# An attention loop whose blocks begin with the scores of the next but one, and a first tile set up in another order

## The chip, the cores and the metric

The kernel runs on one core of a Trainium2 chip. The metric is the device time of one launch in microseconds (us). The core's engines each work through their own instruction stream in order and wait for one another on semaphores: TensorE (PE, with its weight loads as PEld), VectorE (DVE), ScalarE (ACT), GpSimd (POOL) and the DMA queue of SyncE (SP).

## What is computed

Two encoder layers over 512 tokens and 16 learned meta tokens of width 1024. Each layer is wrapped in two gated feed-forward parts; layer 0 mixes by a short convolution and a state-space model, layer 1 by windowed attention with 16 heads, 4 key heads and a head width of 64. Cut to what matters here:

```
def swiglu(x, w_gate, w_up, w_down):
    return (jax.nn.silu(x @ w_gate) * (x @ w_up)) @ w_down

h = h + 0.5 * swiglu(rmsnorm(h, norm_ff1[layer]), ff1_w_gate[layer], ff1_w_up[layer], ff1_w_down[layer])
...
s_band = jnp.einsum('bnqhgd,bnshd->bhgnqs', qr, kb) - slopes * dist
s_meta = jnp.einsum('bnqhgd,bmhd->bhgnqm', qr, km)
probs = softmax_with_sink(jnp.concatenate([s_meta, s_band], axis=-1), sink)
o_real = (jnp.einsum('bhgnqm,bmhd->bnqhgd', probs[..., :N_META], vm)
          + jnp.einsum('bhgnqs,bnshd->bnqhgd', probs[..., N_META:], vb))
out = o_real.reshape(bsz, n_real, N_HEADS * HEAD_DIM)
return out.astype(hn.dtype) @ w_o
```

## The kernel before

Every dense product is made of three matmuls on split operands: a weight `w` becomes `wh` (rounded) and `wl = w - wh`, an input `x` becomes `xh` and `xl`, and PE sums `wh*xh + wh*xl + wl*xh`. A weight unit is 128x2048 values (16 blocks of 128x128). SP loads it into one of two `raw` slots, ACT makes `wh` (`split_high`, L1184), DVE makes `wl` (`split_low`, L1463), and the slot is loaded again when `wl` is done. Everything is written out by hand: the order of the calls in the source is the order in each engine's stream, and nothing overtakes within an engine.

**Start.** PE transposes the input tokens, DVE copies them into `h`. ACT sums the squares of the meta tokens and of the four token tiles (L1264, L1267), makes `wh` of the first tile's gate half (L1270), takes the roots of the sums (L1272), and makes the eight input slices `xh` (L1196), with `wh` of the up half (L1278) after the fifth. DVE makes `wl` of the gate half (L1569), the reciprocals and the eight `xl` (L1484). PE's `first_job` (L762) is the gate tile: 8 steps of k, 3 products each, as two matmuls of 264 columns; it waits for `xl(k)` before any product of step k. Then `first_scale` (L839) spreads the token norms, then the up tile. DVE copies the norms into `r` (L1583) and scales the gate tile into `t_a` (L1516), which frees the gate tile's banks for PE's third tile.

**Attention.** 16 blocks n = 0 to 15, four (j) for each key head (g). In block n before the change:

- PE: `probs_t(n)` transposes the normalised probabilities (L1097, L1098); `scores(n+2)` (L1086, L1087); then dense work, which is a quarter of the query projection of group g+2 (12 matmuls, L1045) while g+2 < 4, and from block 8 on the pieces of the output projection that `fill` names (`out_part(d, k0, k1)`, 3 matmuls of 512 columns for each k, L1141); then `values(n)` (L1108, L1110).
- DVE: `probs_meta(n)` copies the last transpose (L1866), `normed(n+1)` (L1854 to L1861), `softmax(n+2)` (scores and bias L1844, maximum L1848), `out_low(n)` (L1872). In blocks with j = 2 and g+2 <= 4 a whole `split_low` follows.
- ACT: `probs(n)` copies the four transposes (L1415), `exps(n+2)` (four exponentials, L1410), `out_high(n)` (L1420). In blocks 0, 4 and 8 a whole `split_high` follows.

What waits for what: `probs_t(n)` for `normed(n)`; `scores(n)` for the four L1844 of `softmax(n-1)`; `values(n)` for `probs(n)` and `probs_meta(n)`; `normed(n)` for `exps(n)`; `exps(n)` for `softmax(n)`; `out_high(n)` for `values(n)`; `out_low(n)` for `out_high(n)`. `scores(12)` also waits for a query norm that POOL makes from sums in block 8.

The second weight unit of the output projection (WO[0] + 1) is the one whose split falls in blocks 8 and 10; `out_part(2, ...)` in block 14 is the first to read it.

## Time and profile before

| | |
|---|---|
| median of 3 runs | 1949.73 us (1948.42 to 1950.04) |
| the profiled execution's own time | 1950.2 us |
| its span | 1948.1 us |
| PE busy | 1928.7 us, 99% of the span |
| DVE, ACT, POOL busy | 961.0, 604.7, 315.4 us |
| attention blocks 8 to 15 | 1493.33 to 1540.25 us of the span |

The span runs from the first to the last instruction of the profile; what is 2.1 us more in the time lies around it. A busy PE is not a PE at its peak, since a matmul's record lasts as long at half the clock as it needs there; the granted clock (PEclk, 1.00 is full speed) is a column of its own.

### The profile page before, as it was taken

What the parts mean: (1) busy time and instruction counts of PE and PEld (TensorE: products, weight loads), DVE (VectorE), ACT (ScalarE), POOL (GpSimd) and SP (SyncE); (2) the same over time, 40 slices, a digit from 0 to 9 for tenths busy, and PEclk for the clock granted to TensorE, in tenths of its full rate; (3) what the DMA queues carried; (4) which work ended last, traced back from release to release, by engine and by line L of the source; (5) the groups of instructions that cost most, each with busy time, mean ns of one, the idle gap of its engine ahead of it and who ended that gap; (6) DMA issues with size and microseconds to landing.
All of it is one profiled execution on the core that took longest, in us unless ns stands there. A gap on an engine that the chain in (4) does not pass through costs nothing.

```text
span 1948.1 us, 33853 instructions
## 1 busy us (share of the span) xinstructions
PE 1928.7 (99%) x13943; PEld 1813.2 (93%) x13943; DVE 961.0 (49%) x1059; ACT 604.7 (31%) x710; POOL 315.4 (16%) x568
## 2 busy tenths in 40 slices
PE   7999999999999999999999999999999999999999
PEld 7999999999999999999999999999877778888887
DVE  5444367566765443344554433445556554433443
ACT  5222222332243222222342222223455433222222
POOL 2888888001230000000000000000012000000000
PEclk9999999999999999999999999999999899999999
DMA  6322544455333322432243334322311133233323
GB/s 177 87 81 81 152 137 139 129 133 130 96 88 87 86 81 82 118 87 70 79 111 86 82 86 113 87 70 81 108 44 44 44 108 87 78 95 108 101 70 89
DMA packets 329026, 185.61 MB, mean 95 GB/s; under 512 B 7288, under 2 KB 322968, under 8 KB 328952
## 3 DMA queue, kind: packets, MB, share of 16 engines
q1 hardware_dynamic: 323280, 166.81, 30.8%
q0 software_dynamic: 5344, 17.69, 3.2%
q8 instruction: 53, 0.87, 0.2%
q14 instruction: 21, 0.17, 0.0%
q10 hardware_dynamic: 328, 0.07, 0.0%
HBM read 173.56 MB, written 9.80 MB: 94 GB/s over the span
## 4 chain that ended last, share of the span: by engine, by line
PE 96%; DVE 2%; ACT 1%; issue 0%; ACTq 0%
PE ps L729 78%; PE ps L948 5%; PE ps L990 2%; PE ps L1045 2%; PE ps L1009 1%; PE ps L1173 1%; PE ps L1141 1%; ACT arena L1410 1%; DVE wl L1463 0%; PE ps L770 0%; DVE arena L1844 0%; PE ps L1110 0%; PE ps L1108 0%; PE ps L1086 0%; PE ps L883 0%; PE ps L909 0%
## 5 line engine op out<-in xcount | busy, mean ns | idle before, releaser
L729 PE MATMUL ps<-xl,wh 128*128 128x264 f32 (+1 forms) x2448 | 567.1, 301 | 0.0
L729 PE MATMUL ps<-xh,wh 128*128 128x264 f32 (+1 forms) x2448 | 565.9, 301 | 0.1
L729 PE MATMUL ps<-xh,wl 128*128 128x264 f32 (+1 forms) x2448 | 565.7, 301 | 0.0
L1463 DVE TENSOR_TENSOR wl<-raw,wh 128x2048 fp32r<-128x2048 f32 x173 | 411.1, 2376 | 169.8 <-ACT wh L1184 169.6
L729 PEld LDWEIGHTS ps<-xh,wh 128*128 128x128 f32 x2448 | 392.3, 188 | 16.9 <-issue 0.7
L1184 ACT ACTIVATE wh<-raw 128x2048 fp32r<-128x2048 f32 x173 | 329.6, 1905 | 246.7 <-PE ps L729 211.3
L729 PEld LDWEIGHTS ps<-xl,wh 128*128 128x128 f32 x2448 | 391.3, 188 | 15.7 <-issue 0.2
L729 PEld LDWEIGHTS ps<-xh,wl 128*128 128x128 f32 x2448 | 391.0, 188 | 14.9
L729 PE MATMUL ps<-act_l,wh 128*128 128x264 f32 (+1 forms) x1232 | 284.7, 301 | 0.0
L729 PE MATMUL ps<-act_h,wh 128*128 128x264 f32 (+1 forms) x1232 | 284.6, 301 | 0.0
L729 PE MATMUL ps<-act_h,wl 128*128 128x264 f32 (+1 forms) x1232 | 284.3, 301 | 0.0
L1519 DVE TENSOR_TENSOR t_c<-ps,r 128x528 f32<-128x528 f32 (+1 forms) x88 | 61.9, 703 | 371.7 <-PE ps L729 371.6
L729 PEld LDWEIGHTS ps<-act_h,wh 128*128 128x128 f32 x1232 | 197.4, 188 | 7.7
L729 PEld LDWEIGHTS ps<-act_l,wh 128*128 128x128 f32 x1232 | 196.8, 188 | 7.5
L729 PEld LDWEIGHTS ps<-act_h,wl 128*128 128x128 f32 x1232 | 196.6, 188 | 7.5
L1224 ACT ACTIVATE act_h<-t_c 128x528 f32 (+3 forms) x88 | 56.6, 643 | 461.9 <-DVE t_c L1522 461.9
L310 POOL TENSOR_TENSOR arena<-arena 128x32 f32<-128x32 f32 (+7 forms) x245 | 186.3, 760 | 24.8 <-DMA ssm_tables<-arena 5.8
L613 POOL TENSOR_SCALAR arena<-arena 128x16 f32<-128x16 f32 x4 | 1.0, 258 | 899.2 <-DVE arena L1832 863.6
L1499 DVE SCALAR_TENSOR_TENSOR h<-ps,h 128x528 f32 (+2 forms) x72 | 50.7, 704 | 192.6 <-PE ps L729 184.4
L1222 ACT ACTIVATE t_bs<-t_a 128x528 f32<-128x528 f32 (+1 forms) x88 | 56.5, 642 | 282.6 <-DVE t_a L1516 282.6
L1524 DVE TENSOR_TENSOR act_l<-t_c,act_h 128x528 f32 (+3 forms) x88 | 68.6, 779 | 78.9 <-ACT act_h L1224 78.9
L1522 DVE TENSOR_TENSOR t_c<-t_c,t_bs 128x528 f32<-128x528 f32 (+1 forms) x88 | 68.5, 778 | 9.0
(296 smaller groups left out, 1684.0 us busy)
## 6 DMA issues: line engine op xcount, KB each, us to landing
raw<-in_ff_w_gate SPq DMA_DIRECT2D x88, 512.0 KB, 4.0
raw<-in_ff_w_up SPq DMA_DIRECT2D x88, 512.0 KB, 5.2
raw<-in_ff_w_down SPq DMA_DIRECT2D x64, 384.0 KB, 4.0
raw<-in_ff_w_down SPq DMA_DIRECT2D x64, 320.0 KB, 3.7
raw<-in_even_w_in SPq DMA_DIRECT2D x16, 512.0 KB, 5.2
raw<-in_attn_w_qkv SPq DMA_DIRECT2D x12, 512.0 KB, 4.6
raw<-in_even_w_out SPq DMA_DIRECT2D x8, 512.0 KB, 4.6
raw<-in_attn_w_o SPq DMA_DIRECT2D x8, 512.0 KB, 4.7
```

The lines of the kernel that those rows point to most:

```text
L310: did(g.tensor_tensor(o, x, y, op))
L729: last = nc.tensor.matmul(ps[:, 2 * pair + hf, 0:nh], w[:, slot, b * P:(b + 1) * P], x[:, k0 + k, c0 + hf * nh:c0 + (hf + 1) * nh], start= ...
L948: last = nc.tensor.matmul(ps[:, 2 * (p % 2) + hf, 0:L // 2], w[:, slot, b * P:(b + 1) * P], x[:, k, hf * L // 2:(hf + 1) * L // 2], start= ...
L990: last = nc.tensor.matmul(ps[:, 2 * (d % 2) + hf, 0:L // 2], w[:, slot, b * P:(b + 1) * P], x[:, k, hf * L // 2:(hf + 1) * L // 2], start= ...
L1184: nc.scalar.activation(wh[:, c % 2, :], raw[:, c % 2, :], ACT.Copy).then_inc(wh_ready, 1)
L1222: nc.scalar.activation(t_b[:, cols], t_a[:, cols], ACT.Silu).then_inc(silu_done[n], 1)
L1224: nc.scalar.activation(act_h[:, s + 2 * i, cols], t_c[:, cols], ACT.Copy).then_inc(act_h_done[n], 1)
L1463: v.tensor_tensor(wl[:, c % 2, :], raw[:, c % 2, :], wh[:, c % 2, :].bitcast(F32), ALU.subtract).then_inc(wl_ready, 1)
L1499: v.scalar_tensor_tensor(hd, tile(pair, col), scale, hd, ALU.mult, ALU.add).then_inc(tile_evac, 1)
L1519: v.tensor_tensor(halves(t_c, col), tile(1, col), halves(r, col), ALU.mult).then_inc(tile_evac, 1)
L1522: v.tensor_tensor(t_c[:, cols], t_c[:, cols], t_b[:, cols], ALU.mult).then_inc(gated[n], 1)
L1524: v.tensor_tensor(act_l[:, s + 2 * i, cols], t_c[:, cols], act_h[:, s + 2 * i, cols].bitcast(F32), ALU.subtract).then_inc(act_ready[n], 1)
```

## The change

Three things, none of which adds or removes a matmul.

1. **Block order.** PE begins block n with `scores(n+2)`, then a first piece of dense work (`fill`, only in blocks 9 and 12 to 15), then `probs_t(n)`, then the query quarter or the second dense piece (`cover`), then `values(n)`. Blocks 8, 10 and 11 have only the second piece. DVE runs `softmax(n+2)` ahead of `normed(n+1)`; ACT runs `out_high(n)` ahead of `exps(n+2)`.
2. **Split of unit WO[0] + 1.** ACT makes it in two halves at the ends of blocks 8 and 9, DVE in four quarters at the ends of blocks 9 to 12.
3. **First tile.** The gate half is loaded with a semaphore of its own. ACT makes its `wh` before the last square, starts the `xh` slices at once, and takes the roots only after `wh` of the up half. DVE makes `wl` in pieces of 2 and 6 blocks around the first `xl`. PE starts step k on `xh(k)` alone and waits for `xl(k)` only ahead of the second product. `first_scale` moves into the middle of the up tile.

```diff
             def first_job(col):
...
-                pe.wait_ge(gate_split[1], 1)
+                pe.wait_ge(gate_split[0], 1)
                 for k in range(KD):
-                    pe.wait_ge(x_ready, k + 1)
+                    pe.wait_ge(xh_done, k + 1)
                     for q, (w, x) in enumerate(((wh, xh), (wh, xl), (wl, xh))):
+                        if q == 1:
+                            pe.wait_ge(x_ready, k + 1)
+                        if q == 2 and k in (0, EARLY):
+                            pe.wait_ge(gate_split[1], 1 if k == 0 else 2)
...
+            def second_job(col):
...
+                pe.wait_ge(wh_ready, 1)
+                for k in range(KD):
+                    if k == KD // 2:
+                        first_scale()
...
                                 first_job(col)
-                                first_scale()
-                                pe.wait_ge(wl_ready, 1)
+                                second_job(col)
+                                continue
...
-            fill = {8: [(0, 0, 2)], 9: [(0, 2, 4)], 10: [(1, 0, 1)], 11: [(1, 1, 2)], 12: [(1, 2, 4)], 13: [(0, 4, 6)], 14: [(2, 0, 4)], 15: [(1, 4, 6), (2, 4, 6)]}
+            fill = {9: [(0, 2, 3)], 12: [(1, 2, 3)], 13: [(0, 4, 5)], 14: [(2, 0, 2)], 15: [(1, 4, 6)]}
+            cover = {8: [(0, 0, 2)], 9: [(0, 3, 4)], 10: [(1, 0, 1)], 11: [(1, 1, 2)], 12: [(1, 3, 4)], 13: [(0, 5, 6)], 14: [(2, 2, 4)], 15: [(2, 4, 6)]}
             for n in range(NB):
                 g, j = divmod(n, NT)
-                probs_t(n)
                 if n + 2 < NB:
                     scores(n + 2)
+                for d, k0, k1 in fill.get(n, ()):
+                    out_part(d, k0, k1)
+                probs_t(n)
                 sums = g + 1 if j == 0 and g + 1 < NKV else None
                 if g + 2 < NKV:
                     query_part(g + 2, j // 2, j % 2, sums)
-                for d, k0, k1 in fill.get(n, ()):
+                for d, k0, k1 in cover.get(n, ()):
                     out_part(d, k0, k1, sums)
                 values(n)
...
+            def half_high(hf):
+
+                c, at = WO[0] + 1, slice(hf * UNITW // 2, (hf + 1) * UNITW // 2)
+                act.wait_ge(raw_landed[c % 2], 32 * (c // 2 + 1))
+                act.wait_ge(tile_full, j0 + 2 * NKV)
+                nc.scalar.activation(wh[:, c % 2, at], raw[:, c % 2, at], ACT.Copy).then_inc((half_split, wh_ready)[hf], 1)
...
+                out_high(n)
                 if n + 2 < NB:
                     exps(n + 2)
-                out_high(n)
-                if n % NT == 0 and g + 2 <= NKV:
+                if n % NT == 0 and g + 2 < NKV:
 
                     split_high(u0 + 4 + (g + 1) % 2, (g + 1) // 2, j0 + 2 * (g + 2))
+                if n in (NB // 2, NB // 2 + 1):
+                    half_high(n - NB // 2)
...
+                if n + 2 < NB:
+                    softmax(n + 2)
                 if n + 1 < NB:
                     normed(n + 1)
-                if n + 2 < NB:
-                    softmax(n + 2)
...
-                if j == 2 and g + 2 <= NKV:
+                if j == 2 and g + 2 < NKV:
                     split_low(u0 + 4 + (g + 1) % 2, (g + 1) // 2)
+                if NB // 2 < n <= NB // 2 + 4:
+                    quarter_low(n - NB // 2 - 1)
```

Where the streams differ, three places. The first is ACT's stream at the start of the program, from the square of the meta tokens to the norms' diagonals (`t_c`). Before:

```order
15 L1264 ACTIVATE act_l,tok<-arena 16x2x512
16 L1267 ACTIVATE act_l,tok<-arena 128x2x512 x4
17 L1270 ACTIVATE wh<-raw 128x1024
18 L1272 ACT_TABLE_LOAD
19 L1272 ACTIVATE tok<-tok 128x4
20 L1273 ACTIVATE tok<-tok 16x1
21 L1196 ACTIVATE xh<-h,vec 128x528 x5
22 L1278 ACTIVATE wh<-raw 128x1024
23 L1196 ACTIVATE xh<-h,vec 128x528 x3
24 L1281 ACTIVATE t_c<-ident,tok 128x128 x4
```

And in the changed kernel (L1226 is the `xh` slice, L1304 and L1311 the two halves of `wh`):

```order
16 L1299 ACTIVATE act_l,tok<-arena 128x2x512 x3
17 L1304 ACTIVATE wh<-raw 128x1024
18 L1226 ACTIVATE xh<-h,vec 128x528
19 L1299 ACTIVATE act_l,tok<-arena 128x2x512
20 L1226 ACTIVATE xh<-h,vec 128x528 x7
21 L1311 ACTIVATE wh<-raw 128x1024
22 L1313 ACT_TABLE_LOAD
23 L1313 ACTIVATE tok<-tok 128x4
24 L1314 ACTIVATE tok<-tok 16x1
25 L1317 ACTIVATE t_c<-ident,tok 128x128 x4
```

The fourth square, the table load and both roots went behind the input slices. The second place is ACT's stream in blocks 9 and 10 (`arena<-ps` is `probs`, `arena<-arena` the exponentials, `act_h<-ps` is `out_high`). Before, from `probs(9)` on:

```order
392 L1415 ACTIVATE arena<-ps 128x512
393 L1410 ACTIVATE arena<-arena 128x145 x4
394 L1420 ACTIVATE act_h<-ps 128x2x128
395 L1415 ACTIVATE arena<-ps 128x512
396 L1410 ACTIVATE arena<-arena 128x145 x4
397 L1420 ACTIVATE act_h<-ps 128x2x128
```

And in the changed kernel, from `probs(9)` to `probs(10)` and a little around them (L1451 is `probs`, L1456 `out_high`, L1446 the exponentials, L1464 half a split):

```order
390 L1456 ACTIVATE act_h<-ps 128x2x128
391 L1446 ACTIVATE arena<-arena 128x145 x4
392 L1464 ACTIVATE wh<-raw 128x1024
393 L1451 ACTIVATE arena<-ps 128x512
394 L1456 ACTIVATE act_h<-ps 128x2x128
395 L1446 ACTIVATE arena<-arena 128x145 x4
396 L1464 ACTIVATE wh<-raw 128x1024
397 L1451 ACTIVATE arena<-ps 128x512
```

`probs(n)`, for which `values(n)` waits, now stands behind four exponentials and, in blocks 9 and 10, behind half a split. The third place is DVE's stream in block 10 (`arena<-ps` 128x128 is `probs_meta`, `act_l<-ps` is `out_low`). Before:

```order
628 L1866 COPY arena<-ps 128x128
629 L1854 RECIPROCAL arena<-arena 128x4
630 L1860 TENSOR_TENSOR t_c<-arena 128x512
631 L1861 TENSOR_TENSOR arena<-arena 128x4x17
632 L1844 SCALAR_TENSOR_TENSOR arena<-ps,arena 128x145 x4
633 L1848 TENSOR_REDUCE arena<-arena 128x4
634 L1872 TENSOR_TENSOR act_l<-ps,act_h 128x2x128
635 L1463 TENSOR_TENSOR wl<-raw,wh 128x2048
636 L1866 COPY arena<-ps 128x128
```

And in the changed kernel:

```order
632 L1918 COPY arena<-ps 128x128
633 L1896 SCALAR_TENSOR_TENSOR arena<-ps,arena 128x145 x4
634 L1900 TENSOR_REDUCE arena<-arena 128x4
635 L1906 RECIPROCAL arena<-arena 128x4
636 L1912 TENSOR_TENSOR t_c<-arena 128x512
637 L1913 TENSOR_TENSOR arena<-arena 128x4x17
638 L1924 TENSOR_TENSOR act_l<-ps,act_h 128x2x128
639 L1934 TENSOR_TENSOR wl<-raw,wh 128x512
640 L1918 COPY arena<-ps 128x128
```

The softmax went ahead of the normalising, and what stands between `out_low(10)` and `probs_meta(11)` is a quarter of the split instead of the whole.

## Rows read from the trace of the kernel before

**Rows 1.** Chain that ended last: shares by engine; one piece (start, us, line, count).

```profile
PE 96%; DVE 2%; ACT 1%; issue 0%; ACTq 0%
...
1531.24 2.78 PE ps L1141 x12
```

**Rows 2.** PE's waits: line, releaser, us in total, times, longest.

```profile
PE ps L770 <- DVE xl L1484: 6.6, 1, 6.6
PE ps L1108 <- DVE arena L1866: 3.3, 1, 3.3
...
PE ps L1108 <- issue: 0.8, 1, 0.8
PE ps L1086 <- DVE arena L1844: 0.5, 1, 0.5
```

**Rows 3.** Blocks 8, 12, 15: busy us of PE, PEld, DVE, ACT, POOL; PEclk.

```profile
1493.33:1499.81 6.48, 6.48 (x58) 5.42 (x56) 4.24 (x12) 2.60 (x11) 0.00 (x0) 1.00 0.50 138
...
1518.28:1525.79 7.51, 7.51 (x41) 5.91 (x39) 3.48 (x11) 4.16 (x18) 0.00 (x0) 0.58 0.32 89
...
1535.40:1540.25 4.85, 4.85 (x31) 3.75 (x30) 0.62 (x2) 0.98 (x2) 0.00 (x0) 1.00 0.00 0
```

**Rows 4.** Timeline of PE, block 10: start, duration, line, operation.

```profile
1505.56 0.66 PE L1097 MATMUL ps<-ident,t_a 128*128 128x128 f32 x4
...
1506.26 0.50 PE L1086 MATMUL ps<-arena 64*128 64x128 f32 x4
...
1507.28 0.50 PE L1141 MATMUL ps<-act_h,wh 128*128 128x512 f32 x1
...
1508.09 0.38 PE L1108 MATMUL ps<-arena 128*128 128x128 f32 x2
...
1509.56 0.66 PE L1097 MATMUL ps<-ident,t_c 128*128 128x128 f32 x4
```

**Rows 5.** Timeline of DVE, blocks 10 and 11.

```profile
1507.54 0.28 DVE L1866 COPY arena<-ps 128x128 f32<-128x128 f32 x1
...
1508.68 1.19 DVE L1844 SCALAR_TENSOR_TENSOR arena<-ps,arena 128x145 f32<-128x145 f32 x4
1509.90 0.76 DVE L1848 TENSOR_REDUCE arena<-arena 128x4 f32<-128x580 f32 x1
...
1513.04 2.28 DVE L1463 TENSOR_TENSOR wl<-raw,wh 128x2048 fp32r<-128x2048 f32 x1
```

**Rows 6.** Timeline of ACT, block 10: first exponential, copy of block 11.

```profile
1510.69 0.42 ACT L1410 ACTIVATE arena<-arena 128x145 f32<-128x145 f32 x1 [3.05 <-DVE arena L1848]
...
1512.57 0.58 ACT L1415 ACTIVATE arena<-ps 128x512 f32<-128x512 f32 x1
```

**Rows 7.** Timeline of ACT and DVE at the start.

```profile
12.12 1.04 ACT L1267 ACTIVATE act_l<-arena 128x1024 fp32r<-128x1024 f32 x1
...
13.15 1.04 ACT L1270 ACTIVATE wh<-raw 128x1024 fp32r<-128x1024 f32 x1
...
15.71 3.23 ACT L1196 ACTIVATE xh<-h,vec 128x528 fp32r<-128x528 f32 x5
...
16.46 3.48 DVE L1484 SCALAR_TENSOR_TENSOR xl<-h,vec,xh 128x528 fp32r<-128x528 f32 x5 [0.41 <-ACT xh L1196]
...
21.66 1.26 ACT L1281 ACTIVATE t_c<-ident,tok 128x128 f32<-128x128 f32 x4
...
27.98 0.71 DVE L1516 TENSOR_TENSOR t_a<-ps,r 128x528 f32<-128x528 f32 x1
...
33.14 0.71 DVE L1519 TENSOR_TENSOR t_c<-ps,r 128x528 f32<-128x528 f32 x1 [4.45 <-PE ps L729]
```

**Rows 8.** Columns of rows 3: first tile; query projection; blocks 9 to 11.

```profile
17.30:22.50 5.20, 5.13 (x23) 5.16 (x24) 4.61 (x7) 5.20 (x10) 4.92 (x7) 0.50 0.88 151
...
1425.30:1428.70 3.40, 3.40 (x10) 2.67 (x11) 1.69 (x3) 2.49 (x3) 2.18 (x10) 0.54 0.00 0
...
1503.20:1512.20 9.00, 8.19 (x72) 6.07 (x72) 5.32 (x16) 4.67 (x19) 1.08 (x5) 1.00 0.00 0
```

More of the change, by code:

```diff
@@ L29 @@
 UNITW = BLK * P
+EARLY = 2
 def trunk_program(nc, a, out, stop=None):
@@ L764, in first_job @@
                 c0, nh, nb = col
-                pe.wait_ge(gate_split[1], 1)
+                pe.wait_ge(gate_split[0], 1)
                 for k in range(KD):
-                    pe.wait_ge(x_ready, k + 1)
+                    pe.wait_ge(xh_done, k + 1)
                     for q, (w, x) in enumerate(((wh, xh), (wh, xl), (wl, xh))):
+                        if q == 1:
+                            pe.wait_ge(x_ready, k + 1)
+                        if q == 2 and k in (0, EARLY):
+                            pe.wait_ge(gate_split[1], 1 if k == 0 else 2)
                         for hf in range(nb):
                             last = nc.tensor.matmul(ps[:, hf, 0:nh], w[:, 0, k * P:(k + 1) * P], x[:, k, c0 + hf * nh:c0 + (hf + 1) * nh],
+                                                    start=(k == 0 and q == 0), stop=(k == KD - 1 and q == 2))
+                last.then_inc(tile_full, 1)
+            def second_job(col):
+                c0, nh, nb = col
+                pe.wait_ge(wh_ready, 1)
+                for k in range(KD):
+                    if k == KD // 2:
+                        first_scale()
+                    for q, (w, x) in enumerate(((wh, xh), (wh, xl), (wl, xh))):
+                        if k == 0 and q == 2:
+                            pe.wait_ge(wl_ready, 1)
+                        for hf in range(nb):
+                            last = nc.tensor.matmul(ps[:, 2 + hf, 0:nh], w[:, 0, (KD + k) * P:(KD + k + 1) * P], x[:, k, c0 + hf * nh:c0 + (hf + 1) * nh],
                                                     start=(k == 0 and q == 0), stop=(k == KD - 1 and q == 2))
@@ L1273, in _ @@
             nc.scalar.activation(tok[0:META, 0, NT:NT + 1], tok[0:META, 0, NT:NT + 1], ACT.Sqrt).then_inc(sd_ready, 1)
-            act.wait_ge(init_evac, NT + 2)
-            for d in range(KD):
-                scaled_high(0, d, ALL)
-                if d == KD // 2:
-                    nc.scalar.activation(wh[:, 0, GW:2 * GW], raw[:, 0, GW:2 * GW], ACT.Copy).then_inc(wh_ready, 1)
             act.wait_ge(tok_r, 2)
@@ L1572, in _ @@
             v.reciprocal(tok[0:META, 1, NT:NT + 1], tok[0:META, 0, NT:NT + 1]).then_inc(tok_r, 1)
-            for d in range(KD):
-                scaled_low(0, d, ALL)
-            dve.wait_ge(wh_ready, 1)
-            v.tensor_tensor(wl[:, 0, GW:2 * GW], raw[:, 0, GW:2 * GW], wh[:, 0, GW:2 * GW].bitcast(F32), ALU.subtract).then_inc(wl_ready, 1)
             dve.wait_ge(init_evac, NT + 2)
@@ L1873, in out_low, with quarter_low @@
                                 cols(act_h).bitcast(F32), ALU.subtract).then_inc(ol_done, 1)
+            def quarter_low(q):
+                c, at = WO[0] + 1, slice(q * UNITW // 4, (q + 1) * UNITW // 4)
+                if q < 2:
+                    dve.wait_ge(half_split, 1)
+                else:
+                    dve.wait_ge(wh_ready, c + 1)
+                low = v.tensor_tensor(wl[:, c % 2, at], raw[:, c % 2, at], wh[:, c % 2, at].bitcast(F32), ALU.subtract)
+                if q == 3:
+                    low.then_inc(wl_ready, 1)
             dve.wait_ge(prep, count["att_consts"])
```

41 lines of the change are left out of this document (33 added, 8 removed).

## The prediction

> **What bounds the kernel now.** I read the chain of work that ended last first: 96% of it is PE [rows 1], so a change pays only where PE waits or runs at half its clock. The waits of PE are few [rows 2]: 6.6 us for the first `xl`, and in the attention loop 3.3 us in block 11 (`values(11)` for `probs_meta(11)`), 0.8 us in block 9, 0.5 us in block 0. The third view is the granted clock by stretches: 0.50 while the first tile runs [rows 8], and 0.58 in block 12 [rows 3]. Everything else on PE is dense and unchanged, since no matmul is added or removed. So the whole question is how much of these waits and slow stretches goes, and what new waits the new orders make.
>
> **Attention, what goes.** The 3.3 us: DVE starts a whole `split_low` at 1513.04, 2.28 us long, behind `out_low(10)`, and `probs_meta(11)` stands behind it [rows 5]. The quarters take about 0.65 us each (a quarter of 2.28 plus a fixed part), so the wait goes. It costs a second time: after it PE is at 1.2 GHz instead of 2.4. Block 12 takes 7.51 us [rows 3], and its parts at full clock are transposes 0.70, scores 1.02, three dense matmuls 0.81 (six: 0.81 + 3 x 0.23 = 1.50, with 2.78 / 12 = 0.23 for one [rows 1]), values 1.47 [rows 4], together 4.69; that is 2.8 us, and `values(11)` ahead of it, 2.7 us at half speed by the same ratio, lose 1.2. The 0.8 us of block 9 were ACT's whole `split_high` ahead of `probs(9)`; as two halves of 1.04 us (the same copy of 1024 columns [rows 7]) at the ends of blocks 8 and 9 it comes back below. What can go: 3.35 + 0.84 + 4.0 = 8.2 us.
>
> **Attention, what comes.** (a) Block 0. PE now begins with `scores(2)`, which need the four L1844 of `softmax(1)`. They were 0.5 us late when 0.7 us of transposes stood ahead [rows 2, 4]; now the transposes stand behind, and nothing covers: the wait is about 1.2 us, 0.75 more.
>
> (b) ACT. `values(n)` waits for `probs(n)`, and ahead of that ACT now has `out_high(n-1)` and four exponentials, both after `values(n-1)`. These take 1.88 us (1510.69 to 1512.57) and `probs` 0.58 [rows 6]. With 0.1 us until ACT sees `values(n-1)` and 0.05 back to PE, that is 2.6 us from the end of one `values` to the start of the next. PE has, in between, in blocks 10 and 11: scores 1.02, transposes 0.70, three matmuls 0.81 = 2.53, so 0.1 us is missing; in blocks 9, 12, 13 with the first dense piece 3.34, nothing missing; in blocks 1 to 7 a quarter query projection of 12 matmuls (0.81 + 9 x 0.23 = 2.9) makes 4.6, and even in blocks 1 and 5, where a whole `split_high` (about 1.9 us) comes too, ACT's 2.6 + 1.9 = 4.5 just fits. The half splits do not fit: 2.6 + 0.95 = 3.55 against 3.34 in block 9 (0.2 missing) and against 2.53 in block 10 (1.0 missing). Sum: 0.2 + 1.0 + 0.1 = 1.3 us, say 1.4.
>
> (c) DVE. Its block is `probs_meta` and `normed` 1.14 (1507.54 to 1508.68), `softmax` 1.2 + 0.7 [rows 5], `out_low` 0.35, a quarter 0.6: 4.0 us with nothing waited for, against PE's 4.0 us in blocks 10 and 11 (1505.56 to 1509.56) [rows 4]. After `probs_meta(n)` DVE needs 2.9 us until `normed(n+1)` is done; PE then has `values(n)` 1.47 and `scores` 1.02 ahead of the transposes that need it, plus what it waited for ACT (0.3 or more), so about even. I put nothing on it and keep 0.5 us for the range. In blocks 0 to 7 PE's 6.1 us cover it.
>
> (d) More, smaller groups. The first matmul of a dense group takes 0.12 us longer than the others (0.81 for three [rows 4] against 0.23 each [rows 1]). Five blocks (9, 12 to 15) have one group more: 0.5 us.
>
> (e) POOL: `scores(12)` come 0.7 us earlier in their block; the norm for them needs about 5 us from the end of block 8's dense work, and PE gets there 6.4 us later (values 1.5, block 9 4.9). Hidden. `wl` of the second unit is ready in block 12, read in block 14; its slot is loaded two blocks later and read at the end of the output projection. Hidden by some 25 us.
>
> Attention: 8.2 - 0.75 - 1.4 - 0.5 = **5.6 us**. If ACT's and DVE's gaps all close, 7; if they double, 3.7.
>
> **Start.** ACT: the third square ends and the gate copy starts at 12.12 instead of 13.15 [rows 7]; it ends at 13.15, the first `xh` (3.23 / 5 = 0.65 us) at 13.8, the fourth square at 14.8, seven more `xh` at 19.3, the up half of `wh` at 20.3. The table load and the roots take what lay between the gate copy and the first `xh` before, 15.71 - 14.19 = 1.5 us, and DVE's reciprocals 0.3 more, so `t_c` starts at about 22.1 instead of 21.66. The gate half must have landed by 12.1; in the trace its copy starts straight behind the squares, and it is the first load after the tokens, so I take it as landed. PE: `wh*xh(0)` at 13.8 instead of 17.37; `xl(0)` at 14.5; `xh(1)` at 15.4, `xl(1)` at 16.2; from there on ACT and DVE deliver a step each 0.7 us, and PE is the slower one while its clock is half: before, four steps took the 5.2 us of the slow stretch [rows 8], 1.3 us a step, and 0.73 at full clock (six matmuls of 0.23 x 264 / 512 = 0.12). So steps 0 and 1 are done at 17.1 at half clock, or 16.7 at full, against 20.0 before. Then it hangs on when the clock rises. Before, it rose 5.2 us after the matmuls began. In the query projection it was at half for 3.4 us of dense matmuls [rows 8] and then full. From the dense stream's start at 16.2 that gives 19.6 to 21.4; I take 19.5, because sparse work from 13.8 on lies ahead of it. Then 1.8 steps are done at half by 19.5, and 4.2 x 0.73 = 3.1 remain: the gate tile ends at 22.5 instead of 25.5, **3.0 us** earlier. At 22.7 it would be 24.0, 1.5 us; with no fall at all `xl(7)` (20.4) bounds it.
>
> The up tile follows without a wait (`wh` 20.3, `wl` 21.6) and holds the 1.4 us of `first_scale` that stood in front of it; `t_c` is complete at 23.7, needed at 25.4. The next bound is the third tile, which needs the gate tile scaled into `t_a`. Before, that came 6.3 us after the start of `t_c` (21.66 to 27.98), through ACT's and DVE's split of the next unit, and no PE wait lies in it. It will be at 28.4, done at 29.1. The third tile starts after the up tile at 22.5 + 5.85 + 1.4 = 29.8 instead of at about 32.9 (DVE is released at 33.14 [rows 7]). So 3.0 us is kept, and 3.8 is the most there can be. Behind it PE is dense for hundreds of us, so the gain stays.
>
> **A page that speaks against it.** Between dense pieces PE will have values, scores and transposes in one row, with short waits. Blocks 9 to 11 had just that with a wait of 0.84 us, and the granted clock stayed at 1.00 up to 1512.2 [rows 8]. The Trainium skill, "TensorE: Matmul & The Clock Gate", section "A second HAM failure mode: psum-queue depth-cycling", says that a PE which idles briefly but often between groups of matmuls lets its clock oscillate between half and full. By the page blocks 9 to 13 would be partly slow, and the sum would be worth 4 us less or worse; by the row it stands.
>
> **Sum.** 5.6 + 3.0 = 8.6 us from a time of 1950.2 us for the profiled execution (span 1948.1): 1941.6. The median is 0.5 below that execution, so **1941.1 us**, -0.44%. A measurement of this kernel can tell about 0.2% (3.9 us) from no change. The likeliest case alone runs from 1939.5 (start 3.6, attention 6.6) to 1944.1 (start 1.5, attention 4.1).
>
> **Rivals.**
> 1. *The clock falls once in the thinned stretch or behind block 0's 1.2 us wait.* For it: before the query projection PE waited for nothing and still ran at 0.54 behind transposes and two-column matmuls; block 0 now has 1.2 us of waiting and 1.7 of small matmuls in a row. Against: rows 8, blocks 9 to 11. Price: as in blocks 11 and 12, 4.0 us: 1945.1. Chance 0.14.
> 2. *The early start is lost.* The sparse products do not count, and the clock rises at 22.7 or later, as before. For it: the clock was at 0.50 when the first tile began. Attention is unchanged: 5.6 + 0.5 to 1.5, 1942.6 to 1943.6. Chance 0.11.
> 3. *The wait moves to `normed`.* DVE's softmax stands ahead of it, and each of blocks 9 to 13 makes the transposes wait. By (c) the loop of DVE is 4.0 us, as long as PE's; with 0.6 us of semaphores in each of five blocks that is 3 us: 1944. Against: the exponentials are done before DVE comes to them. Chance 0.06.
> 4. *Slower: the clock falls in block 9 and does not come back until block 13's end.* A slow block took 7.51 against 4.69, 1.6 times. Blocks 9 to 13 hold 4.8 + 4.0 + 4.0 + 4.8 + 4.8 = 22.4 us of PE work; 0.6 of that is 13.4, less the 1.4 of waits that disappear in it: 12 us lost, 8.6 gained, 1953. It decides from 14 us of PE work at half clock on. For it: only 0.8 to 1.6 us of each 4 to 5 is dense. Against: block 10 had as little and kept 1.00. This is what the page's rule would do here at its worst. Chance 0.04.
> The forecast itself has 0.65.
>
> **Range and chances.** 1938.5 to 1946 holds the forecast, rivals 2 and 3 and most of rival 1. Below 1945.8 lie the forecast, rivals 2 and 3 and some two thirds of rival 1, less what I may have overlooked: faster 0.85, within 0.2% 0.10, slower 0.05.
>
> **What would show it.** In the changed trace: L1135 in block 11 without a wait of more than 0.3 us and clock 1.00 in blocks 11 and 12; a wait of about 1 us ahead of `values(10)` with `probs` as its releaser, 0.2 in block 9; a wait of about 1.2 us for `scores(2)`; blocks 8 to 15 in 40.5 us instead of 46.9; the first product at 13.8; PE at full clock by 20; the up tile's release of DVE at about 30. Wrong if the gate half lands after 12.1, if blocks 1 and 5 wait for `probs` (0.1 us of margin), or if the clock falls where it did not.

## The result, and the profile after

On the same chip the changed kernel took **1937.97 us** (median of 6 runs, 1937.42 to 1941.06) and the kernel before 1949.93 us (6 runs, 1948.42 to 1951.09): ratio 0.9941, 95% interval 0.9928 to 0.9954. The forecast was 1941.1 us with a range of 1938.5 to 1946, so the median lies 0.5 us below the range. The direction and most parts were right; the gain was 12.0 us where 8.6 was summed. The profiled execution after took 1938.08 us, its span is 1936.3 (before 1950.2 and 1948.1).

The shares of the chain that ended last, and PE's waits (line, releaser, us in total, times, longest), which answer to [rows 1, 2]:

```profile
PE 98%; DVE 1%; ACT 0%; DMA 0%; issue 0%; SPq 0%
```

```profile
PE ps L782 <- ACT xh L1226: 2.2, 1, 2.2
PE ps L1135 <- issue: 1.7, 3, 1.1
...
PE ps L1113 <- DVE arena L1896: 1.1, 1, 1.1
```

The 3.3 us of block 11 are gone. `values` (L1135) waits three times, 0.4 us in block 9, 1.1 in block 10, 0.2 in block 11; the forecast had 0.2, 1.0 and 0.1. Block 0's wait is 1.1 us, where 1.2 was forecast. "issue" hides the releaser here, and the timeline of ACT, from `out_high(9)` to `probs(10)`, names it (start, duration; L1456 is `out_high`, L1464 half the split, L1451 `probs`); the last line is PE's `values(10)`:

```profile
1499.74 0.38 ACT L1456 ACTIVATE act_h<-ps 128x256 fp32r<-128x256 f32 x1 [1.76 <-PE ps L1137]
...
1501.62 1.05 ACT L1464 ACTIVATE wh<-raw 128x1024 fp32r<-128x1024 f32 x1
1502.57 0.58 ACT L1451 ACTIVATE arena<-ps 128x512 f32<-128x512 f32 x1
...
1503.24 0.46 PE L1135 MATMUL ps<-arena 128*128 128x128 f32 x2 [1.14 <-issue]
```

`probs` ends at 1503.15 and `values(10)` starts at 1503.24. In experiment 7, where no half split stands there, block 10 takes 4.22 us instead of 5.16.

Stretches of PE: first tile mostly at half clock, then the rest of the first two tiles, the query projection, the end of block 9 with most of block 10, and block 12 (columns as in rows 3):

```profile
14.40:18.30 3.90, 3.66 (x15) 3.17 (x16) 3.87 (x8) 3.90 (x7) 3.90 (x5) 0.56 0.85 150
18.30:29.70 11.40, 11.40 (x93) 11.21 (x93) 7.71 (x12) 8.59 (x15) 4.42 (x6) 1.00 0.78 170
1422.40:1428.05 5.65, 5.65 (x26) 4.33 (x26) 1.69 (x3) 2.37 (x3) 3.27 (x15) 1.00 0.00 0
...
1498.90:1504.90 6.00, 4.86 (x46) 3.51 (x45) 5.32 (x15) 3.40 (x11) 0.00 (x0) 1.00 0.00 0
...
1509.10:1513.90 4.80, 4.76 (x41) 3.52 (x41) 3.83 (x12) 2.58 (x10) 0.00 (x0) 1.00 0.00 0
```

Block 12 is at 1.00 and takes 4.8 us, where it took 7.51 at 0.58 [rows 3]. In the query projection the clock is 1.00, where it was 0.54 for 3.4 us [rows 8]; the change edits nothing in that stretch, and the forecast had counted on no difference.

PE's and ACT's timelines at the start:

```profile
14.40 0.48 PE L782 MATMUL ps<-xh,wh 128*128 128x264 f32 x2 [2.25 <-ACT xh L1226]
15.12 0.81 PE L782 MATMUL ps<-xl,wh 128*128 128x264 f32 x2 [0.24 <-DVE xl L1529]
...
22.43 0.41 PE L797 MATMUL ps<-xh,wh 128*128 128x264 f32 x2
...
25.35 1.05 PE L870 MATMUL ps<-t_c,ones 128*128 128x128 f32 x8
...
29.70 0.48 PE L737 MATMUL ps<-xh,wh 128*128 128x264 f32 x2
```

```profile
11.81 1.04 ACT L1304 ACTIVATE wh<-raw 128x1024 fp32r<-128x1024 f32 x1
13.52 0.73 ACT L1226 ACTIVATE xh<-h,vec 128x528 fp32r<-128x528 f32 x1 [0.67 <-DVE vec L1608]
...
19.59 1.05 ACT L1311 ACTIVATE wh<-raw 128x1024 fp32r<-128x1024 f32 x1
...
22.53 1.28 ACT L1317 ACTIVATE t_c<-ident,tok 128x128 f32<-128x128 f32 x4 [0.28 <-DVE tok L1628]
```

The first product comes at 14.40 (forecast 13.8), since ACT waits 0.67 us for DVE's copy of the vectors. The clock is full from 18.3 on (19.5), the gate tile ends at 22.43 (22.5), `t_c` starts at 22.53 (22.1), and the third tile starts at 29.70 (29.8). That the gate tile ends on time is two errors that cancel: the first product came 0.6 us later than forecast, and the full clock 1.2 us earlier.

**Where the 11.8 us of span went.** From the start times of PE's pieces in the two timelines (before, after):

| stretch | before | after | gained |
|---|---|---|---|
| start to the key transposes | 1422.23 | 1419.20 | 3.03 |
| key transposes to `scores(0)` | 10.32 | 8.78 | 1.54 |
| `scores(0)` to `scores(1)` | 4.02 | 4.01 | 0.01 |
| `scores(1)` to the end of block 0 | 12.39 | 12.89 | -0.50 |
| blocks 1 to 7 | 44.37 | 43.30 | 1.07 |
| blocks 8 to 15 | 46.85 | 40.28 | 6.57 |

A block ends here where the next piece of PE starts, so blocks 8 to 15 before are 46.85 us and not the 46.9 that runs to the end of `values(15)`. The sum is 11.72. Two lines were not in the forecast at all: 1.54 in the query projection and 1.07 in blocks 1 to 7.

### The profile page after: what moved, and what is told of

It is laid out like the page before. It is cut to its first block, busy times and chain, and to the rows that moved or that the text cites. A ratio compares the mean times of both kernels' runs of the same rounds, so it can differ in the third digit from the quotient of the medians.

```text
span 1936.3 us, 33860 instructions
## 1 busy us (share of the span) xinstructions
PE 1922.4 (99%) x13943; PEld 1808.8 (93%) x13943; DVE 959.7 (50%) x1063; ACT 605.2 (31%) x711; POOL 317.6 (16%) x568
## 4 chain that ended last, share of the span: by engine, by line
PE 98%; DVE 1%; ACT 0%; DMA 0%; issue 0%; SPq 0%
PE ps L737 78%; PE ps L975 5%; PE ps L1017 2%; PE ps L1072 2%; PE ps L1036 1%; PE ps L1168 1%; PE ps L1203 1%; PE ps L1135 1%; PE ps L1137 1%; PE ps L1113 1%; PE ps L1124 0%; PE ps L782 0%; PE ps L910 0%; PE ps L936 0%; PE ps L935 0%; PE ps L926 0%
## 5 line engine op out<-in xcount | busy, mean ns | idle before, releaser
L1220 ACT ACTIVATE t_bs<-h 128x528 f32 (+1 forms) x40 | 25.7, 644 | 147.8 <-DVE h L1544 129.4
```

## The experiments

Medians are of the runs beside the kernel before on the same chip; a gain read from a stretch is from the profiled execution.

**1. The kernel before, unchanged.** How far do executions differ?

> The kernel before, unchanged, to see the granted clock of several executions. Theory A (the fall of the clock behind the key transposes is a matter of chance and of when PE gets there): at least one of its executions shows it missing, its mean clock is then 0.996 instead of 0.995 and its time about 1.6 us lower. Theory B (the change itself took it away): every execution has it, and the 24 matmuls of the second query half take 7.3 us as in the first profile, never 5.7.

1949.94 us (10 runs, 1947.43 to 1950.40), ratio 0.9999 (0.9990 to 1.0009). The 27 runs of the kernel before on that chip reach from 1947.31 to 1951.27, with none between 1948.9 and 1949.4. So a single profiled execution can stand 2 us above or below another of the same kernel. In the profile the query projection's clock fell again. Three of the ten executions lie at 1947.4 to 1948.2 with a mean clock of 0.996, as theory A wants; but three at 1949.8 to 1950.3 have 0.996 too, so the times alone don't settle it. The profiles of 2, 3 and 4 do: they have no fall, and 3 and 4 keep the start of before.

**2. The start alone.** `first_job`, `second_job`, the loads and the streams of ACT and DVE at the start; the attention loop of before.

```
+            def second_job(col):
...
-                pe.wait_ge(gate_split[1], 1)
+                pe.wait_ge(gate_split[0], 1)
```

> The first tile's new order alone. My sum: 3.0 us faster than before (the trace of the changed kernel shows the third tile 3.15 us earlier); a rival that the early products bring no earlier clock gives 0.5 to 1.5 us. The attention loop keeps its waits of 3.3, 0.8 and 0.5 us and its half clock of 9 us. If the clock behind the key transposes depends on the moment at which PE arrives there, this run may have lost that fall too and be 4.6 us faster.

1946.82 us (1944.93 to 1948.59), 2.8 us below the median before. Stretches from the first product to full clock, and of blocks 11 and 12:

```profile
13.50:19.00 5.50, 4.86 (x22) 4.18 (x23) 5.47 (x10) 5.50 (x10) 5.50 (x6) 0.69 1.01 198
...
1511.70:1520.30 8.60, 8.59 (x40) 6.54 (x41) 6.13 (x18) 2.71 (x11) 0.00 (x0) 0.50 0.44 123
```

The start's gain stands by itself, and the 3.3 us wait with half the clock behind it stays in the attention loop. In the profile the key transposes start 2.3 us earlier than in the kernel before, not 3.0.

**3. The order of the blocks alone.** PE's, ACT's and DVE's order of the changed kernel, with the whole splits of before.

```
-                probs_t(n)
                 if n + 2 < NB:
                     scores(n + 2)
+                for d, k0, k1 in fill.get(n, ()):
+                    out_part(d, k0, k1)
+                probs_t(n)
```

> The block order of all three engines alone, with the unit's split still whole at the ends of blocks 8 (ACT) and 10 (DVE). By the streams: block 0 waits 1.1 us; blocks 1 to 7 gain 1.1 us, since a dense group behind transposes costs 0.2 us less than one behind the scores; the wait in block 9 is about 1.1 us, in block 11 about 0.9, and neither is long enough for the clock to fall: 6 us faster than before. A rival that the whole split alone makes the long wait (3.3 us) and the fall behind it gives at most 2 us.

1942.33 us (1941.39 to 1943.08), ratio 0.9965 (0.9952 to 0.9977). Blocks 8 to 15 take 41.1 us, and their clock is 1.00. The whole split costs `values` one wait of 1.2 us and one of 1.0, instead of 3.3 and a slow stretch. The medians give the order 7.3 us. The stretches give it 6.3: 5.8 in blocks 8 to 15 and 1.05 in blocks 1 to 7, less 0.5 in block 0, where 6 was expected.

**4. The splits alone.** Halves and quarters, orders and start of before.

```
+                if n in (NB // 2, NB // 2 + 1):
+                    half_high(n - NB // 2)
...
+                if NB // 2 < n <= NB // 2 + 4:
+                    quarter_low(n - NB // 2 - 1)
```

> The halves and quarters alone, all streams in the order of before. The loop through DVE and ACT then has a period of 5.5 us a block (the copies of the last transposes stood at 1496.5, 1502.0 and 1507.5), and PE has 4.0 us of work in blocks 10 and 11 and 4.7 in 12 and 13: waits of about 1 us each stay in blocks 11 to 13, but no long one, and the clock stays at 1.00: 4 us faster. A rival that the whole split is all that was wrong gives 7 us or more.

1948.53 us (1945.80 to 1949.53), ratio 0.9995 (0.9986 to 1.0005). A miss: it was expected some 4 us faster. PE's wait (L1109 is `values`, L1876 `probs_meta`), the stretch from `values(10)` to the end of block 11's scores, and ACT's first exponential of block 9:

```profile
PE ps L1109 <- DVE arena L1876: 4.5, 4, 1.7
```

```profile
1506.10:1516.70 10.60, 8.92 (x69) 6.24 (x69) 6.51 (x18) 4.37 (x20) 0.00 (x0) 0.84 0.01 2
```

```profile
1502.56 0.42 ACT L1411 ACTIVATE arena<-arena 128x145 f32<-128x145 f32 x1 [2.12 <-DVE arena L1858]
```

The 3.3 us wait did not go, it was dealt out: 4.5 us in four blocks. Nor did the clock stay at 1.00, as was expected: behind the longest of these waits, 1.7 us ahead of `values(11)`, it was 0.50 from 1512.2 to 1515.6. Blocks 8 to 15 take 45.5 us, 1.4 less than before. With the old order ACT's exponentials wait for a softmax that stands behind DVE's `normed`, and `out_high`, the half split and `probs` wait behind them. In the kernel before, the whole `split_low` was only what stood visibly in front of `probs_meta`.

**5. The changed kernel again**, as the base of 6 to 8, on another chip.

> The changed kernel once more. The kernel before falls into two groups of times, about 1947.9 and 1950.2 us, and the second is the one in which the clock falls behind the key transposes. If that fall is chance in any kernel, the changed kernel has the same two groups about 10 us lower, near 1937.9 and 1940.2. If the change takes the fall away, there is one group near 1937.9 alone.

1940.51 us (1939.55 to 1941.82), kernel before 1949.05, ratio 0.9954 (0.9938 to 0.9971). The waits are those of the first profile. But in the query projection the clock fell:

```profile
1422.60:1425.90 3.30, 3.30 (x10) 2.62 (x10) 1.69 (x3) 2.50 (x3) 2.07 (x10) 0.50 0.00 0
1425.90:1429.90 4.00, 4.00 (x19) 2.97 (x17) 0.00 (x0) 0.00 (x0) 1.23 (x6) 0.99 0.00 0
```

From the sums to `scores(0)` it took 9.09 us, in the first profile of the changed kernel 7.51. Same program, same place: the 1.5 us of the table above come with the execution, not with the change.

**6. Block 0's transposes ahead of `scores(2)`**, as they stood before.

```
+                if n == 0:
+                    probs_t(n)
                 if n + 2 < NB:
                     scores(n + 2)
...
+                if n:
+                    probs_t(n)
```

> The changed kernel with the transposes of block 0 ahead of scores(2), as they stood before. My reading: the wait for the scores in block 0 goes from 1.1 us to 0.5, so 0.7 us faster than the changed kernel; nothing else moves. A rival that the wait hides other late work (POOL's query norm) gives no gain.

1939.49 us (1938.26 to 1940.86), ratio 0.9949. The wait is 0.5 us instead of 1.1, and `scores(1)` to block 8 takes 55.7 us instead of 56.2: 0.5 us, for the wait that term (a) had priced at 0.75. The wait itself is 0.7 us shorter; the other 0.2 is a border between transposes and scores that comes back with the old order (see below).

**7. Both halves of ACT's split in block 8**, where 12 matmuls of the query projection give ACT time.

```
-                if n in (NB // 2, NB // 2 + 1):
-                    half_high(n - NB // 2)
...
+                if n == NB // 2:
+                    half_high(0)
+                    half_high(1)
                 out_high(n)
```

> The changed kernel with both halves of ACT's split made in block 8 between the copy of the transposes and the output copy, where ACT stands idle for almost 4 us, instead of at the ends of blocks 8 and 9. If the exponentials plus half a split ahead of the copy are what values(9) and values(10) wait for, the waits of 0.4 and 1.1 us shrink to 0.2 us or less each: 1.3 us faster than the changed kernel. A rival that DVE's order (softmax ahead of normalising) sets the pace of blocks 9 to 11 keeps waits of about 0.5 us there: under 0.7 us.

1938.78 us (1938.33 to 1939.79), ratio 0.9946 (0.9929 to 0.9962). Waits of the attention loop:

```profile
PE ps L1113 <- DVE arena L1897: 1.1, 1, 1.1
PE ps L1135 <- issue: 0.4, 2, 0.2
```

1.7 us of waits of `values` became 0.4, and blocks 8 to 15 take 39.0 us instead of 40.3. So the half splits made the wait of block 9 and all but 0.2 us of block 10's. What is left, 0.19 us each in blocks 10 and 11, is not theirs; there ACT still has `out_high` and four exponentials ahead of `probs`.

**8. Edits 6 and 7 together.**

> Both edits: the gains add, 2.0 us faster than the changed kernel, about 1935.9 us in the group without the clock's fall. A rival that they share a wait gives 1.3.

1938.20 us (1937.40 to 1938.79), ratio 0.9940 (0.9923 to 0.9957): 2.3 us below the changed kernel on that chip. The stretches show that the gains add: 0.5 us in block 0 and 1.3 in blocks 8 to 15, 1.8 in all, where the rival had 1.3.

**9. All dense pieces behind the transposes.** The tables are those of before in the new order.

```
-            fill = {9: [(0, 2, 3)], 12: [(1, 2, 3)], 13: [(0, 4, 5)], 14: [(2, 0, 2)], 15: [(1, 4, 6)]}
+            fill = {}
```

> The changed kernel with every dense piece of blocks 9 and 12 to 15 behind the transposes, none ahead of them. My term (d) as it stood: five groups fewer at 0.12 us each, 0.5 us faster. The reading of the changed kernel's trace (a group of three costs 0.70 us behind the transposes and 0.90 behind scores): also faster, 0.2 us a block from that alone, about 1.0 us. Rival, the piece ahead is there to cover normed(n): then the transposes of blocks 9, 12 and 13 come 0.7 us after scores(n+2) instead of 1.6, wait for DVE by up to 0.5 us each, and the kernel is 0.5 us slower to equal. The count of transposes' waits for DVE's L1912 or L1913, none in the changed kernel, tells them apart.

1940.47 us (1939.87 to 1940.89), ratio 0.9953 (0.9940 to 0.9967). Blocks 8 to 15 take 40.07 us instead of 40.28, so both numbers that I had put on it (0.5 and 1.0) are too large, but each for a reason that the timeline gives. Blocks 12 and 13 are 4.50 us each instead of 4.82 and 4.81; blocks 14 and 15 are 0.05 shorter without their wait; block 9 is unchanged; and the transposes of block 14 wait 0.44 us for `normed(14)`, since their cover is gone, which takes back 0.5 us. Here is block 12 of the changed kernel: dense, transposes, dense, `values`, next `scores`.

```profile
1510.02 0.50 PE L1168 MATMUL ps<-act_h,wh 128*128 128x512 f32 x1
...
1510.83 0.60 PE L1124 MATMUL ps<-ident,t_a 128*128 128x128 f32 x4
...
1511.29 0.48 PE L1168 MATMUL ps<-act_h,wh 128*128 128x512 f32 x1
...
1512.27 0.46 PE L1135 MATMUL ps<-arena 128*128 128x128 f32 x2
...
1513.82 0.39 PE L1113 MATMUL ps<-arena 64*128 64x128 f32 x2
```

The three matmuls behind the transposes take 0.98 us until `values(12)`, the three ahead of them 0.81. The waits of PE do not list it, but those of its weight loads do:

```profile
1512.24 0.30 PEld L1135 LDWEIGHTS ps<-arena 128*128 128x128 f32 x2 [0.44 <-DVE arena L1918]
```

`values(12)` stands so close behind the transposes that their copies are not done.

**10. PE's new order with the old orders of ACT and DVE.**

```
-                out_high(n)
                 if n + 2 < NB:
                     exps(n + 2)
+                out_high(n)
...
-                if n + 2 < NB:
-                    softmax(n + 2)
                 if n + 1 < NB:
                     normed(n + 1)
+                if n + 2 < NB:
+                    softmax(n + 2)
```

> The changed kernel, but ACT runs the exponentials ahead of out_high and DVE runs normed ahead of softmax, as before the change; PE's new order, the splits and the start stay. If the three orders belong together (PE's scores(n+2) stand ahead of the transposes, so softmax(n+2) is free to run while PE does the transposes, and normed only has to be ready behind the first dense piece), the old orders make probs(n) wait for exponentials that wait for DVE: waits of some 0.5 to 1 us ahead of values in blocks 9 to 13, 3 us slower than the changed kernel, 1941 to 1944. Rival, PE's order does it alone: the same time within 1 us, blocks 8 to 15 in 40.3 us.

1945.73 us (11 runs, 1944.10 to 1948.54), ratio 0.9981 (0.9972 to 0.9990). PE's waits in the attention loop:

```profile
PE ps L1135 <- DVE arena L1918: 3.3, 3, 1.7
PE ps L1113 <- DVE arena L1896: 3.0, 6, 1.1
PE ps L1168 <- issue: 0.5, 1, 0.5
```

7.1 us of waits in all, block 0's 1.1 among them. The clock fell once:

```profile
1498.00:1513.00 15.00, 12.37 (x95) 8.93 (x93) 10.71 (x31) 6.73 (x23) 1.82 (x7) 0.89 0.01 2
```

It was 0.50 from 1506.7 to 1510.1, behind the longest wait, 1.7 us ahead of `values(10)`. The median is 5 us above the 1940.51 and 1940.09 that the changed kernel took when measured again (5 and 14), where 3 were expected. The three orders are one edit: PE's alone brings 1.2 us in blocks 8 to 15 against the kernel before, where all three bring 6.6.

**11. The kernel before with the query sums spread.** 8 sums behind the third dense matmul, 8 behind the sixth.

```
+                    if (g, t, k) in ((1, 0, 0), (1, 0, 1)):
+                        query_sums(0, 4 * k, 4 * k + 4)
...
             keys_t()
-            query_sums(0)
```

> The kernel before, with the 16 two-column sums of group 0 given out in two pieces of 8 behind the third and the sixth dense matmul of the query projection instead of in one row ahead of it. If that row (1.8 us of two-column products behind 1.2 us of transposes) is what lets the clock fall, the granted clock of the query projection is 1.00, the 27 matmuls after the transposes take 7.5 us instead of 9.1, less up to 0.8 us that scores(0) may wait for POOL's norm, and the executions lie in one group at 1947 to 1949 instead of two. Rival, the fall is a matter of chance whatever stands there: two groups as before, the profiled clock at 0.5 to 0.7 in some executions.

1949.95 us (11 runs, 1949.26 to 1950.36), ratio 1.0000 (0.9991 to 1.0009). The query projection's stretch, and PE's wait for POOL's norm:

```profile
1423.40:1431.60 8.20, 7.63 (x44) 6.22 (x42) 2.69 (x7) 4.92 (x7) 3.30 (x15) 1.00 0.01 2
```

```profile
PE ps L1088 <- POOL arena L621: 0.6, 1, 0.6
```

Half a hit. The clock is 1.00 there and the 11 runs lie within 1.1 us, where the 21 of the kernel before beside them spread over 3.3. But they lie at the upper end of those, not at the lower one: the median has gained nothing. The stretch says why in the main: from the key transposes to `scores(0)` this kernel takes 9.34 us, with the wait, where the 14 profiles with the sums in one row take 10.3 to 10.4 with the fall and 8.8 without it. Spreading saves 1.0 us in one half of the executions and costs 0.55 in the other. What the rest of the median hangs on is open.

**12. Kernel 8 with the sums spread.**

> The changed kernel with block 0's transposes ahead of scores(2), both halves of ACT's split in block 8, and the sums spread as in the kernel before with its sums spread. If the row of sums lets the clock fall: 1936.5 to 1937.5, all executions within 1 us. If scores(0) waits 0.8 us for the norm and the fall is chance: 1938 to 1940, as without the spreading or slower.

1938.07 us (1937.50 to 1940.42), ratio 0.9943. No gain over kernel 8 either. Its profiled execution has the query projection at 1.00 but the first tile at half clock until 21.8 us, and its third tile starts at 31.62 instead of 29.70: the start has a chance of its own.

**13. Kernel 8 with blocks 9, 12 and 13 whole behind the transposes**, 14 and 15 divided. **14. The changed kernel beside it.**

```
-            fill = {9: [(0, 2, 3)], 12: [(1, 2, 3)], 13: [(0, 4, 5)], 14: [(2, 0, 2)], 15: [(1, 4, 6)]}
+            fill = {14: [(2, 0, 2)], 15: [(1, 4, 6)]}
```

> The changed kernel with block 0's transposes ahead of scores(2), both halves of ACT's split in block 8, and the dense pieces of blocks 9, 12 and 13 whole behind the transposes (14 and 15 stay divided). Theory, the divided piece costs by thin cover: with three matmuls between the transposes and values(n), values waits for the copies of the transposes by 0.2 to 0.3 us, with six it does not. Then blocks 9, 12 and 13 take 4.5 us each instead of 4.82, blocks 8 to 15 take 38.1 us instead of 39.0, and transposes(14) do not wait, since their dense piece still stands ahead of them. Rival, the divided piece is what covers normed(n): blocks 10, 13 and 14 then wait for DVE at their transposes, 0.4 us each as in the kernel with all pieces behind, and blocks 8 to 15 stay at 39.0 or more. The median would be 1937.3 by the theory and 1938.2 by the rival, which the differences between executions could hide; the stretch decides.

> The changed kernel itself, a third time, for comparison on the same chip. Blocks 8 to 15 in 40.3 us. The time lies between the two medians that it gave before, 1937.97 and 1940.51; how far it lies from the best version there is the start's and the query projection's clock, not the blocks.

**1937.17 us** (1935.81 to 1938.96), ratio 0.9935 (0.9921 to 0.9948), against 1940.09 (1938.05 to 1941.14), ratio 0.9949 (0.9935 to 0.9963), for the changed kernel. Blocks 8 to 15 take 38.00 us (expected 38.1) and 40.27. Block 12 of kernel 13:

```profile
1510.22 0.66 PE L1124 MATMUL ps<-ident,t_a 128*128 128x128 f32 x4
...
1510.74 0.48 PE L1168 MATMUL ps<-act_h,wh 128*128 128x512 f32 x1
...
1512.22 0.38 PE L1135 MATMUL ps<-arena 128*128 128x128 f32 x2
```

Six matmuls in 1.48 us and no wait for the copies: thin cover it was. No transposes wait for `normed`. This is the fastest kernel of the study, 2.9 us below the changed one, of which the stretches show 2.8 (0.5 in block 0, 2.3 in blocks 8 to 15).

The profile of 14 shows what the start can do. Its first tile, and the start of its third:

```profile
15.00:22.00 7.00, 6.81 (x31) 6.42 (x31) 6.96 (x12) 6.98 (x11) 7.00 (x9) 0.52 0.83 138
...
31.30 0.40 PE L737 MATMUL ps<-xh,wh 128*128 128x264 f32 x2
```

The clock is half until 21.7 instead of 18.3, and the third tile starts 1.6 us later than in the first profile of the same kernel.

## Why the prediction was right, and where it was wrong

**Right.** More than half of the gain is the 3.3 us wait of block 11 and the slow clock behind it, and both went. Blocks 8 to 15 were forecast at 40.5 us and measured 40.28, and 40.27 when repeated. The waits on ACT (0.4, 1.1 and 0.2 for 0.2, 1.0 and 0.1) came from its queue, counted instruction by instruction, and experiment 7 took 1.3 of these 1.7 us away by moving only the half splits.

**Right in part by luck: the start.** It was forecast at 3.0 us and gave 3.03 in this pair of profiles. But over the eleven profiles with the new start the key transposes begin between 1419.2 and 1421.1, over the five with the old one between 1421.1 and 1422.3, and the two medians (1419.9 and 1422.2) are 2.3 us apart. The pair that was compared is the earliest of the new ones and one of the latest of the old ones. Two things make the difference. The half-speed stretch in the first tile lasts 3.4 us in eight of the eleven, and the third tile then starts at 29.5 to 30.4; it lasts 6.8 us in three (8, 12 and 14), and the third tile starts at 30.6 to 31.6. And "PE is dense for hundreds of us, so the gain stays" does not always hold: in 2, 6 and 7 PE waits 0.5 to 0.65 us for DVE's `t_a` at about 326 us, and 1 us of the gain is lost on the way.

**The failed step: "Everything else on PE is dense and unchanged, since no matmul is added or removed."** It put nothing on two stretches that gave 2.6 of the 3.1 us between the sum (8.6) and the table (11.7): the query projection, 1.54 us, of which more below, and blocks 1 to 7, where no wait goes and which gained 1.07 us. Without either of the two the median would have been inside the range. The other 0.5 us is block 0 (0.50 lost for 0.75) and blocks 8 to 15 (6.57 for 6.3).

In blocks 1 to 7 the gain comes with PE's order: experiment 3, with the start and the splits of before, has it too (43.32 us), and in experiment 10, with the old orders of ACT and DVE, the blocks without a wait take 5.88 to 5.90 us. PE's weight loads show how. Their groups over those blocks (busy us, mean ns, and idle time ahead of them with its cause), in the kernel before, from 1448.9 to 1493.3:

```profile
L1086 PEld LDWEIGHTS ps<-arena 64*128 64x128 f32 x56 | 4.4, 185 | 1.2 <-issue 1.2
...
L1097 PEld LDWEIGHTS ps<-ident,t_c 128*128 128x128 f32 x16 | 1.7, 141 | 0.7 <-issue 0.7
L1097 PEld LDWEIGHTS ps<-ident,t_a 128*128 128x128 f32 x12 | 1.3, 140 | 0.5 <-issue 0.5
```

and in the changed kernel, from 1444.8 to 1488.1:

```profile
L1113 PEld LDWEIGHTS ps<-arena 64*128 64x128 f32 x56 | 4.4, 186 | 1.2 <-issue 1.2
...
L1124 PEld LDWEIGHTS ps<-ident,t_c 128*128 128x128 f32 x16 | 1.7, 140 | 0.1
L1124 PEld LDWEIGHTS ps<-ident,t_a 128*128 128x128 f32 x12 | 1.3, 140 | 0.1
```

Before, the weight loads stood idle 0.17 us (1.2 / 7) at two borders of each block (and at one inside `values`, which both kernels have): from `values` to the transposes and from the transposes to the scores. Now there is one, from `values` to the scores, and from the scores to the transposes there is none. It is worth 0.2 us in each of blocks 2, 3, 4, 6 and 7 (6.10 to 5.88 in block 2). Blocks 1 and 5 gained next to nothing (0.01 and 0.05): there ACT's whole split stands ahead of `probs`, and `values` start 0.1 us later behind their dense work than in block 2. That is a small wait for `probs`, one of the three signs of being wrong that the prediction gave. In experiment 10, where ACT keeps its old order, these two blocks take 5.90 us. Block 8, which no term of the sum touched, gained 0.2 us as well (6.48 to 6.28), so the hit on blocks 8 to 15 is in part luck: waits of 1.7 us for 1.4 stand against borders that were not counted. The row to see it by was in hand: the transposes took 0.70 us to the scores [rows 4], and I used that number for the new order, where they take 0.52 to the dense work (block 2):

```profile
1451.96 0.66 PE L1124 MATMUL ps<-ident,t_a 128*128 128x128 f32 x4
...
1452.48 0.48 PE L1072 MATMUL ps<-xh,wh 128*128 128x512 f32 x1
```

In experiment 3, the order alone, the idle time ahead of the transposes is down to the same 0.1 and 0.1.

The Trainium skill, "TensorE: Matmul & The Clock Gate", section "Step-by-step: what each phase is for", says that weight loads are pulled ahead of running matmuls when their row groups do not conflict or when they go to the background weight buffer. Inside a dense group the trace agrees: the load for the matmul that starts at 1446.73 begins at 1446.50, while the matmul of 1446.41 (0.48 us) still runs. So "nothing overtakes within an engine", as was said of the kernel before, holds for the matmuls and not for the weight loads. The first load of each group starts with its matmul, for scores (1444.87 and 1444.88), transposes (1445.89 and 1445.90) and dense work (1446.39 and 1446.41) alike, so no run here tells which of the page's two conditions fails at the borders that cost 0.17 us. That the borders cost time and which do is shown; why they do is not.

**Term (d)** gave 0.12 us to each of five divided pieces. The sum was near (experiment 9: 0.3, 0.3, 0.05, 0.05 and nothing), the cause was another: division costs little in itself, but three matmuls between the transposes and `values` do not cover the copies. Where six do, in blocks 14 and 15, it is 0.05. After the first trace I had read the term as having the wrong sign; experiment 9 refuted that.

**Not foreseen: which execution the profile shows.** The profile before had the clock's fall in the query projection, the one after had not: 1.5 us of the difference. Of the 14 profiles with the sums in one row seven had the fall (the kernel before, 1, 5, 8, 9, 13 and 14), with the orders of before and of the change alike; neither of the two with the sums spread had it. Two profiles could be chance; that the 11 executions of experiment 11 lie within 1.1 us, less than the 1.5 of a fall, speaks for a cause in that row. And the third tile of the new start came between 29.49 and 31.62 us in different executions. Three measurements of the changed kernel gave 1937.97, 1940.51 and 1940.09; the 15 runs together have a median of 1939.93 and lie in two groups, 1937.4 to 1938.6 and 1939.5 to 1941.8. Against those 15 runs the forecast is off by 1.2 us, about the 1.07 of the failed step. But that agreement is no proof: the three gains over the kernel before were 12.0, 8.5 and 9.6 us, where the sum had 8.6. What the 1.07 rests on is the stretch: 44.37 us in all five profiles with the old order, 43.30 to 43.33 in all ten with the three new orders. That the first median fell below the range is this gain and favourable executions together.

**The rivals.** All four were slower cases; none stood on the side on which the median fell out of the range. The clock did not fall in blocks 0 to 15 in any profile of the changed kernel (three of them), though PE waits 1.1 us in block 0 and 1.7 us over blocks 9 to 11, so rivals 1 and 4 did not come. The Trainium skill's rule ("TensorE: Matmul & The Clock Gate", section "A second HAM failure mode: psum-queue depth-cycling") would have had it swing there; this trace does not show that. Over all 16 profiles the clock fell in the loop during or behind each of the six single waits of 1.7 us or more (3.3 to 3.4 us four times, 1.7 in experiments 4 and 10), and behind none of those of 1.3 us and less. Rival 2, the early start lost, did not come in the first profile but did in part in experiment 14: the clock was full only from 21.7 on, and the key transposes began 1.5 us before those of the kernel before, the upper end of the 0.5 to 1.5 that rival 2 had left for the start. Rival 3, a wait for `normed`, is real, but only when its cover is taken away (0.44 us, experiment 9).

Left open: why the clock falls in the query projection in some executions and not in others, and what of the medians of 11 and 12 the wait for POOL's norm does not explain.

## What to carry to other kernels

Price the borders between kinds of matmul, not only the matmuls: a piece costs by what stands behind it, and a new order is worth the difference even where nothing waits (here 0.2 us a block where nothing else takes it back). When an order moves on one engine, move it on all that feed it, and give each copy enough dense work behind its source (here six matmuls, not three) before its reader comes. And take the spread of executions from several profiles before an effect of 1 or 2 us is claimed or a baseline is read from one.

## What the hardware did that I had not expected

- The granted clock fell to about half (0.54 and 0.50 in the two stretches shown) for 3.4 us in the query projection with no wait of PE ahead of it, behind 1.2 us of transposes and 1.8 us of two-column matmuls, in seven of 14 profiled executions of programs that are alike there. With the sums dealt out among dense matmuls, in neither of two.
- A weight load that follows another kind of tile starts 0.17 us late at some borders (`values` to transposes, `values` to scores, transposes to scores) and not at others (scores to transposes, transposes to dense).
- Waits of 0.4, 1.1 and 0.2 us in consecutive blocks left the clock at 1.00, and so did 1.2, 0.2 and 1.0 us in experiment 3; one single wait of 1.7 us in experiments 4 and 10 was followed by 3.4 us at 0.50.
- The half-speed stretch in the first tile lasted 3.4 us in eight profiles of the new start and 6.8 in three, with the same instructions.
